# First MLP's last down stage: the weights' low part made by an accumulating DMA onto ScalarE's negated high part

## What is computed

```python
h = rms_norm(x, norm_mlp_g[l]) @ w_mlp_up[l]              # 256 x 8192
x = x + jnp.square(jax.nn.relu(h)) @ w_mlp_down[l]        # 8192 x 2048
```

## Time and profile before

| | |
|---|---|
| median of 3 runs | 2451.59 us (2451.31 to 2454.28) |
| profiled execution, span | 2449.6 us |
| median less span | 2.0 us |
| PE busy | 2440.3 us, 100% |
| DVE busy | 1797.3 us, 73% |
| ACT busy | 1237.2 us, 51% |
| POOL busy | 61.2 us, 2% |
| DMA | 467.18 MB, mean 191 GB/s |

### The profile page before, as it was taken

How to read it: one execution, slowest core, us unless ns; L and a number is a source line. 1 busy time by engine, 2 the same in 40 slices (tenths; PEclk the granted TensorE clock), 3 DMA queues, 4 the chain that set the end, 5 groups by cost and what they waited for, 6 DMA issues and landing times.

```text
span 2449.6 us, 28947 instructions
## 1 busy us (share of the span) xinstructions
PE 2440.3 (100%) x11683; PEld 2041.8 (83%) x11683; DVE 1797.3 (73%) x1732; ACT 1237.2 (51%) x1314; POOL 61.2 (2%) x67
## 2 busy tenths in 40 slices
PE   9999999999999999999999999999999999999999
PEld 8888888888888888888888888788888888888887
DVE  5775587777755785876775558886788878887887
ACT  5545544445444444444444457875554444545543
POOL 0410000000000000000000000000300000000000
PEclk9999999999999999999999999999999999999999
DMA  8555466666655565565656556445555565656654
GB/s 256 173 186 177 166 191 201 193 204 194 237 189 188 185 205 189 196 195 184 205 189 190 205 182 194 140 155 167 176 191 198 196 203 182 205 200 194 201 189 155
DMA packets 233907, 467.18 MB, mean 191 GB/s; under 512 B 14192, under 2 KB 25984, under 8 KB 233390
## 3 DMA queue, kind: packets, MB, share of 16 engines
q1 hardware_dynamic: 232222, 460.09, 57.7%
q10 hardware_dynamic: 1552, 5.25, 0.6%
HBM read 463.20 MB, written 2.10 MB: 190 GB/s over the span
## 4 chain that ended last, share of the span: by engine, by line
PE 97%; DVE 2%; issue 0%; ACT 0%; POOL 0%; DMA 0%; ACTq 0%; DVEq 0%; POOLq 0%
PE acc L1723 13%; PE acc L1719 13%; PE acc L1720 13%; PE acc L459 10%; PE acc L450 10%; PE acc L452 10%; PE acc L479 5%; PE acc L485 2%; PE tp L479 2%; PE sd L479 2%; PE acc L1777 2%; PE acc L1774 2%; PE acc L1773 2%; PE tp L485 1%; PE sd L485 1%; PE sd L1774 1%
## 5 line engine op out<-in xcount | busy, mean ns | idle before, releaser
L435 DVE TENSOR_TENSOR wlo<-raw,whi 128x2048 fp32r<-128x2048 f32 (+1 forms) x384 | 870.7, 2269 | 524.6 <-ACT whi L427 523.9
L427 ACT ACTIVATE whi<-raw 128x2048 fp32r<-128x2048 f32 (+1 forms) x384 | 725.1, 1890 | 792.1 <-PE acc L1723 335.3
L1719 PE MATMUL acc<-whi,opA_hi 128*128 128x512 f32 x840 | 327.1, 389 | 0.0
L1720 PE MATMUL acc<-whi,opA_lo 128*128 128x512 f32 x840 | 326.8, 389 | 0.0
L450 PE MATMUL acc<-whi,opA_hi 128*128 128x512 f32 x768 | 304.7, 397 | 0.0
L452 PE MATMUL acc<-whi,opA_lo 128*128 128x512 f32 x768 | 299.4, 390 | 0.0
L1723 PE MATMUL acc<-wlo,opA_hi 128*128 128x512 f32 x840 | 225.1, 389 | 0.1
L1719 PE MATMUL acc<-whi,opB 128*128 128x512 f32 x536 | 209.5, 391 | 0.0
L1720 PE MATMUL acc<-whi,opB 128*128 128x512 f32 x536 | 208.6, 389 | 0.0
L459 PE MATMUL acc<-wlo,opA_hi 128*128 128x512 f32 x768 | 192.6, 392 | 0.2 <-DVE wlo L435 0.2
L1723 PEld LDWEIGHTS acc<-wlo,opA_hi 128*128 128x128 f32 x840 | 157.6, 188 | 33.2 <-DVE wlo L435 0.5
(11 more groups left out here) (421 smaller groups left out, 3626.4 us busy)
## 6 DMA issues: line engine op xcount, KB each, us to landing
raw<-in_w_in SPq DMA_DIRECT2D x66, 1024.0 KB, 5.4
raw<-in_w_mlp_up SPq DMA_DIRECT2D x64, 1024.0 KB, 5.4
raw<-in_w_mlp_down SPq DMA_DIRECT2D x64, 1024.0 KB, 5.0
raw<-in_w_in SPq DMA_DIRECT2D x120, 512.0 KB, 4.7
raw<-in_w_gate SPq DMA_DIRECT2D x88, 512.0 KB, 3.8
raw<-in_w_up SPq DMA_DIRECT2D x88, 512.0 KB, 4.7
raw<-in_w_down SPq DMA_DIRECT2D x88, 512.0 KB, 4.6
raw<-in_w_out SPq DMA_DIRECT2D x32, 1024.0 KB, 5.0
```

The costliest lines, as they stand in the source:

```text
L427: eng.activation(whi[:, j % SPL, k, 0:cols], raw[:, j, k, 0:cols], ACT.Copy).then_inc(hi_split, share(k))
L435: eng.tensor_tensor(wlo[:, j % SPL, k, 0:cols], raw[:, j, k, 0:cols], whi[:, j % SPL, k, 0:cols].bitcast(F32), ALU.subtract).then_inc(lo_s ...
L1719: pe.matmul(acc[:, b, m, :], hi[:, 2 * v + a, rows], whi[:, s, 2 * a + b, :], start=first and a == 0, stop=False)
L1720: pe.matmul(acc[:, b, m, :], lo[:, 2 * v + a, rows], whi[:, s, 2 * a + b, :], start=False, stop=False)
```

## The change

In the last down stage alone, the low part is no longer made by VectorE from `raw` and `whi`. ScalarE makes a second copy of `raw`, negated and rounded, into one of `ADD_RING` = 3 slots of a new tensor `added_lo` (`low_begin`), two units ahead of `hi_unit`. GpSimd then issues two DMAs of 512 KB for the unit that read the same weights again from HBM and add them onto `added_lo`, so that -hi becomes w - hi. VectorE only waits for them and counts `lo_split` up. TensorE reads `added_lo` where it read `wlo`. The three slots lie where `seven_hi` and `seven_lo` of the stages before lay, and `low_begin` waits until TensorE is done with all units ahead of the stage. The scratch for GpSimd's DMA descriptors grows from 1024 to 2048 bytes.

```diff
+ADD_RING, ADD_AHEAD = 3, 2
...
+        added_lo = at("added_lo", c1 + 8, [P, ADD_RING, UK, NW], F32R)
...
+            for k in range(UN * UN):
+                pool.wait_ge(lo_begun, k + 1)
+                n, j = k // UN, k % UN
+                for h in range(2):
+                    kt = QUARTERS * KT + UK * j + 2 * h
+                    pool.dma_start(added_lo[:, k % ADD_RING, 2 * h:2 * h + 2, :], w_dn[:, kt:kt + 2, chunk(n)],
+                                   accum_op=ALU.add).then_inc(lo_added[k % ADD_RING], 16)
             pool.wait_ge(staged, 8 * MT)
...
+            def low_begin(k):
+
+                if k >= UN * UN:
+                    return
+                act.wait_ge(landed[k % RAW], loads_before(G_DLAST + k // UN + 1) * 16)
+                act.wait_ge(units_used, G_DLAST * UN + max(k - ADD_RING + 1, 0))
+                act.activation(added_lo[:, k % ADD_RING], raw[:, k % RAW], ACT.Copy, scale=-1.0).then_inc(lo_begun, 1)
+
+            for k in range(ADD_AHEAD):
+                low_begin(k)
             for n in range(UN):
                 for j in range(UN):
                     hi_unit(act, G_DLAST + n, j)
+                    low_begin(n * UN + j + ADD_AHEAD)
                     if n == 0 and j == 0:
...
-                    products(G_DLAST + n, R_DLAST + n, j, opA_hi, opA_lo, UK * j)
+                    products(G_DLAST + n, R_DLAST + n, j, opA_hi, opA_lo, UK * j, low=added_lo[:, (n * UN + j) % ADD_RING])
...
-                    lo_unit(dve, G_DLAST + n, j)
+                    dve.wait_ge(hi_split, ((G_DLAST + n) * UN + j + 1) * HV)
+                    dve.wait_ge(lo_added[(n * UN + j) % ADD_RING], ((n * UN + j) // ADD_RING + 1) * 32)
+                    dve.sem_inc(lo_split, HV)
...
-    nc = bacc.Bacc("TRN2", target_bir_lowering=False, num_devices=1, dynamic_dma_scratch_size=1024)
+    nc = bacc.Bacc("TRN2", target_bir_lowering=False, num_devices=1, dynamic_dma_scratch_size=2048)
```

More of the change, by code:

```diff
@@ L134, in build @@
         base = -(-nc.sbuf_base // 32) * 32
-        room = (nc.sbuf_usable_end - base) // KB - 1
+        room = (nc.sbuf_usable_end - base) // KB
         ctx.enter_context(nc.sbuf_tensor("arena", [P, room * 256], F32))
@@ L286, in build @@
         units_used = sem("units_used")
+        lo_begun = sem("lo_begun")
+        lo_added = [sem(f"lo_added{k}") for k in range(ADD_RING)]
         read_act = sem("read_act")
@@ L436, in lo_part, with unit_products @@
                               whi[:, j % SPL, k, 0:cols].bitcast(F32), ALU.subtract).then_inc(lo_split, share(k))
-        def unit_products(eng, group, j, pair, hi, lo, kt, first, last, cols=NW, mid=None):
+        def unit_products(eng, group, j, pair, hi, lo, kt, first, last, cols=NW, mid=None, low=None):
             s = j % SPL
+            low = wlo[:, s] if low is None else low
             for k in parts(group):
@@ L458, in unit_products @@
                     for m in range(MT):
-                        mm = eng.matmul(acc[:, pair, m, 0:cols], hi[:, kt + i, m * P:(m + 1) * P], wlo[:, s, i, 0:cols],
+                        mm = eng.matmul(acc[:, pair, m, 0:cols], hi[:, kt + i, m * P:(m + 1) * P], low[:, i, 0:cols],
                                         start=False, stop=last and i == UK - 1)
@@ L1494, in _, with products @@
         def _(pe):
-            def products(group, run, j, hi, lo, kt, mid=None):
+            def products(group, run, j, hi, lo, kt, mid=None, low=None):
                 if j == 0:
                     pair_free(pe, run)
-                unit_products(pe, group, j, run % 2, hi, lo, kt, j == 0, j == UN - 1, mid=mid)
+                unit_products(pe, group, j, run % 2, hi, lo, kt, j == 0, j == UN - 1, mid=mid, low=low)
             def stage_operand(c, before, staged_by):
```

## The result

The changed kernel takes 2522.5 us (median of 4, 2521.4 to 2522.7) against 2452.0 us for the kernel before: slower, by a ratio of 1.0287, 95% interval 1.0275 to 1.0299. That is 70.5 us more, where the forecast said 44.4: inside the range 2456 to 2550, but above the 2488 to 2508 that were given for rival A alone. The profiled execution has a span of 2519.7 us, 70.1 us over that of before.

A forecast was written before the change was run, and what follows sets the result against it. TensorE's matmul stream was taken to bound the kernel, with DMA setting the stage's pace after the change: 47 L - 83.4 = +44.4 us (the beginning's 5.9 inside) on 2451.6 gives 2496; range 2456 to 2550.

The forecast's parts named there:

- rival A: Last down stage: an add costs about two loads and DMA sets the pace, +36 to +56 us; chance 0.45.
- TensorE is the bound and VectorE's relief is worth nothing: Last down stage: TensorE busy for 90.70 of 90.70 us, so removing VectorE's 16 subtractions of 2.29 us gains 0.
- Rival E: Without VectorE's subtractions matmuls speed up, giving back up to 5.1 us; decides under 0.2145 us distance; chance 0.05.
- B: An add costs as much as a load, so the beginning's stall decides: +5.9 us, about 2458; chance 0.25.
- 5.9 us at the beginning: Stage's start: two negated copies ahead of unit 0's `whi` move TensorE's first matmul from 1346.38 to 1352.23.
- rival D: TensorE's clock falls to the 1.2 GHz level in the new pauses: all through the stage +93 us, 2545; chance 0.10.
- An add costs 2L, L = 2.72: L is the DMA engines' time in us for 1024 KB; add plus load take 8.2 us a unit against TensorE's 5.44.
- 47 L - 83.4: The stage's added time, from 47 L of DMA work after the first negated copy: +44.4 us at L = 2.72.
- The sign "near 385 GB/s": Expected in the stage from unit 1 or 2 on: both DMA queues together near 385 GB/s, share near 1.0.
- C: An add costs three loads or more, or GpSimd's descriptor making does: +77 to +103 us, 2540; chance 0.15.
- the 4.1 at which it would decide: GpSimd sets the pace once one issue of 512 KB takes over 4.1 us, half of rival A's pace.
- The other `room` and scratch sizes cost no time.: In the changed kernel, the new `room` sizes and GpSimd's descriptor scratch size were put at 0 us.

The follow-up runs named there:

- the plain copy's run: The change, but GpSimd's DMAs copy the weights into `added_lo` and add nothing, so the low part is w: 2460.8 us, ratio 1.0037.
- the run of the copies alone: Against the kernel before, only ScalarE's 16 negated copies added; no DMA from GpSimd, VectorE subtracts as before: 2460.0 us, ratio 1.0033.
- the runs with the engines kept full: The change with 3072 bytes of descriptor scratch in place of 2048, 2495.1 us; the change with four 256 KB DMAs a unit, 2497.3 us.

## Why the prediction was right, and where its number was off

The mechanism came true: DMA-bound, by an add that costs two loads. The number did not: 26 us are missing, and a unit took 9.6 us where 8.2 were worked out. That the result still lies in the range is luck in part, as the range reached to 2550 for three loads and for the lower clock, and neither was the cause.

- **TensorE is the bound and VectorE's relief is worth nothing**: right. No version with the adds, with 16 or 8 subtractions taken off VectorE, came out under the kernel before. Rival E (faster matmuls) has nothing for it: with no subtraction in the stage, in the plain copy's run, the units are 5.44 us apart as before. Its threshold was also worked out wrong: with B at +5.9 and 4.9 us that can't be told from no change, 1 us over 384 matmuls would have done, a distance of 0.224 and not 0.2145.
- **5.9 us at the beginning**: right, 5.9 measured in the run of the copies alone. Left out there: 2.3 us of half clock behind the pause, which belonged to rival D.
- **An add costs 2L, L = 2.72**: right, 5.2 us and 2.75 us (1.9 L), or 5.5 and 2.46 us (2.2 L) at the other bound. The sum 47 L - 83.4 gave 2496; the runs with the engines kept full gave 2495.1 and 2497.3. The sign "near 385 GB/s" was worked out wrong: two times 1024 KB in 8.2 us are 256 GB/s as the profile counts bytes, and 262 were measured. Rivals B and C fall: a copy costs 1 L and would have been free, and three loads' price (2540) is not reached by the runs with full engines. GpSimd's issue takes 1.2 us, well under the 4.1 at which it would decide.
- **The step that failed** is "The other `room` and scratch sizes cost no time." The scratch is what the adds' descriptors stand in. It was put at nothing without a row. At 2048 bytes it holds three DMAs of 512 KB; the next pair is issued only when a unit has landed, with one DMA left in the queue. That is the missing term: 9.60 - 7.98 = 1.6 us a unit, 26 us in all, and 27.4 us between the change and the run with 3072 bytes.
- **Rival D**: the clock did fall, to a mean of 0.86 from 1358.7 to 1495 us, and behind most waits of 3 to 4 us matmuls start 0.43 us apart (1371.47 to 1371.90, with the wait of 3.41 us ahead of 1367.89). The Trainium skill describes this pattern (TensorE: Matmul & The Clock Gate, HAM oscillation), and the trace agrees. It did not decide. The chain that ended last runs from unit 1 on through GpSimd's issues and the adds, with TensorE's matmuls in it only before the first add and after the last. That the lower clock cost nothing there is read from this chain; no run held the clock fixed to show it.

## What to carry to other kernels

Before work is moved onto the DMA engines, count their time per stage like any engine's: a plain second reading of 1024 KB every 5.44 us was free, the same reading as an accumulate took about twice as long on the engines and made DMA the bound, with nothing to win since VectorE was never waited for. Here the depth of GpSimd's queue of accumulates was set by its descriptor scratch. Waits for "issue" in front of its DMAs together with dips of the DMA rate at each issue were the sign that it was too small; DMAs of half the size helped as much as more scratch (2497.3 and 2495.1 us). Where a lookahead is begun at the head of a stage, look at what is queued behind its first wait: the pause costs itself and the clock behind it, and its removal helps only if what it begins can land in time.

## What the runs showed of the hardware

- An accumulating DMA of 512 KB takes GpSimd 1.2 us to issue, a plain one 0.72 (a pair 2.44 and 1.43 us).
- Adds alone moved about 205 GB/s, adds with loads always beside them 262, plain copies with loads 381, which was all that TensorE's pace asked for.
- Three steps of descriptor scratch (1024, 2048, 3072 bytes) let GpSimd issue 1, 3 and 5 adds of 512 KB before its first wait for room, and gave 15.0, 9.6 and 8.0 us a unit.
- After a pause of 5.75 us TensorE's matmuls started 0.43 us apart, in place of 0.227, for 4.8 us.
